# HGRN input projections: the load of the first half of the value weights moved ahead of the last three gate tiles in SyncE's queue

## The reference

```python
def prep(hh):
    p = (hh @ w_in).astype(jnp.float32)
    q, zf, zb, i, g = jnp.split(p, [HG_F, 2 * HG_F, 3 * HG_F, 3 * HG_F + HG_V], axis=-1)
    ff = lb[0] + (1.0 - lb[0]) * jax.nn.sigmoid(zf)
    fb = lb[1] + (1.0 - lb[1]) * jax.nn.sigmoid(zb)
    ...
q, i, g, (lf, kf), (lbk, kb) = prep(h)
```

## Time and profile before

| | |
|---|---|
| median of 3 runs | 2569.86 us (2567.46 to 2570.39) |
| the profiled execution | 2569.05 us |
| its span, first to last instruction | 2567.3 us |
| mean granted TensorE clock over the span | 0.988 |
| PE busy over the span | 2343.3 us, 91% |
| DMA over the span | 949.72 MB, mean 370 GB/s |

### The profile page before, as it was taken

The page is one execution under the profiler, slowest core; times in us unless marked ns, Lnnn a source line. Parts: engine busy times, 40 slices in busy tenths (PEclk is TensorE's granted clock), DMA queues, the critical chain, the costliest instruction groups (busy, mean ns, idle before and its releaser), DMA issues. The chain is left out here.

```text
span 2567.3 us, 25469 instructions
## 1 busy us (share of the span) xinstructions
PE 2343.3 (91%) x7682; PEld 1277.6 (50%) x7682; DVE 1729.9 (67%) x4248; ACT 1154.5 (45%) x3146; POOL 884.3 (34%) x802
## 2 busy tenths in 40 slices
PE   9999999999998999899999998899999888888786
PEld 4787445543553434454545444478755433333222
DVE  4866988876667666757676766564547666666665
ACT  2352568754545444534444444411424444444444
POOL 0000444443444434434444444100114444444442
PEclk9999999999999999999999999999999999999999
DMA  9433999999999999999999999595069999999997
GB/s 370 139 106 113 417 425 426 408 426 427 404 425 427 426 426 414 427 426 426 425 419 424 426 425 427 225 368 205 30 240 391 427 427 427 427 426 427 427 426 320
DMA packets 146682, 949.72 MB, mean 370 GB/s; under 512 B 16496, under 2 KB 22128, under 8 KB 44272
## 3 DMA queue, kind: packets, MB, share of 16 engines
q0 software_dynamic: 112608, 834.72, 77.6%
q1 hardware_dynamic: 33936, 113.37, 11.9%
HBM read 946.98 MB, written 1.05 MB: 369 GB/s over the span
## 5 line engine op out<-in xcount | busy, mean ns | idle before, releaser
L1123 PE MATMUL pY<-uv,diag 128*128 128x512 f32 x3072 | 1450.0, 609 | 183.0 <-ACT diag L1201 181.8
L1356 DVE SCALAR_TENSOR_TENSOR uv<-uv,H 128x1024 f32<-128x1024 f32 x768 | 939.8, 1224 | 559.9 <-DMA uv<-uv_dram,idx 558.5
L1005 POOL DMA_INDIRECT uv<-uv_dram,idx x768 | 862.4, 1123 | 1279.6 <-PE pY L1123 1087.1
L1123 PEld LDWEIGHTS pY<-uv,diag 128*128 128x128 f32 x3072 | 556.3, 191 | 948.7 <-issue 507.3
L1193 ACT ACTIVATE gelu<-dots 128x1 f32<-128x1 f32 x768 | 154.9, 202 | 891.9 <-DVE uv L1356 890.5
L1201 ACT ACTIVATE diag<-cst,coef 128x128 f32<-128x128 f32 x768 | 308.4, 402 | 72.1 <-ACT coef L1197 1.5
L1197 ACT ACTIVATE coef<-gelu,gate 128x1 f32<-128x1 f32 x768 | 226.3, 295 | 28.1 <-ACT gelu L1193 0.4
L1028 PE MATMUL pqs<-hT,wring 128*128 128x256 f32 x512 | 115.6, 379 | 0.7 <-ACT S L1176 0.7
L127 PE MATMUL plh<-hT,wring 128*128 128x256 f32 x512 | 112.5, 380 | 1.6 <-PEq L71 1.6
L1028 PEld LDWEIGHTS pqs<-hT,wring 128*128 128x128 f32 x512 | 97.2, 190 | 26.8 <-issue 15.2
L127 PEld LDWEIGHTS plh<-hT,wring 128*128 128x128 f32 x512 | 96.7, 190 | 15.9 <-issue 2.9
(11 more groups left out here) (450 smaller groups left out, 2145.2 us busy)
## 6 DMA issues: line engine op xcount, KB each, us to landing
wring<-peer_q_dram SPq DMA_DIRECT2D x36, 512.0 KB, 11.4
arena<-ada_w_dram POOLq DMA_DIRECT2D x8, 2048.0 KB, 10.7
wring<-w_in_dram SPq DMA_DIRECT2D x24, 512.0 KB, 3.6
aw<-ada_w_dram POOLq DMA_DIRECT2D x6, 2048.0 KB, 9.9
uv<-uv_dram,idx POOLq DMA_INDIRECT x768, 14.7
arena<-ada_w_dram SPq DMA_DIRECT2D x12, 1024.0 KB, 9.1
arena<-hg_zz_dram SPq DMA_DIRECT2D x16, 512.0 KB, 7.9
wring<-hg_zz_dram SPq DMA_DIRECT2D x16, 512.0 KB, 8.5
```

The source lines that it names most:

```text
L1005: nc.gpsimd.indirect_dma_start(out=uv[:, n % SLOTS, :], out_offset=None, in_=t[f"uv{l}"], in_offset=bass.IndirectOffsetOnAxis(ap=idx[:, s ...
L1123: last = nc.tensor.matmul(pY[:, b, half * 512:(half + 1) * 512], diag[:, n % DIAGS, :], uv[:, n % SLOTS, D + half * 512:D + (half + 1) * 512],
L1356: v.scalar_tensor_tensor(out=uv[:, j, 0:D], in0=uv[:, j, 0:D], scalar=1.0, in1=H2[:, own, :], op0=ALU.mult, op1=ALU.mult, accum_out=dots[: ...
```

## The change

The load of the first half of `wi` is issued behind gate tile 12, the thirteenth, and ahead of tiles 13, 14 and 15. Nothing else is different.

```diff
                 @block.sync
                 def _(sp):
-                    for i in range(RING, 16):
+                    for i in range(RING, 13):
                         load_tile(sp, "hg_zz", i, first[5] + i)
                     sp.dma_start(wi[:], t["hg_i"][:, :, 0:512]).then_inc(s_wi, 16)
+                    for i in range(13, 16):
+                        load_tile(sp, "hg_zz", i, first[5] + i)
                     lin_ahead(sp, 5)
```

## The result

| | before | changed |
|---|---|---|
| median | 2568.81 us (10 runs, 2565.09 to 2571.32) | 2575.72 us (10 runs, 2574.29 to 2578.91) |
| span of the profiled execution | 2567.3 us | 2574.6 us |
| ratio to the kernel before | | 1.0032, 95% interval 1.0024 to 1.0040 |

The ratio is +8.2 us (6.2 to 10.3); the two medians of the table stand 6.9 us apart. The change is slower by more than the 0.2% of a measurement. I had put the likeliest value at +4.7 us, slower by over 0.2% at 0.47, and a change of at most 0.2% either way at 0.50.

The account below looks back on a forecast made before the run. TensorE's chain was taken to bound the phase, with DMA scarce. Tile 13 at 1714.4 + 12.3 + 1.3 clock + 13.8 ends values(0) at 1741.8 against 1737.1: +4.7 us, forecast 2574.5 us, range 2571 to 2579.5.

Parts of the forecast that it names:

- Step 1: SP's queue: wi's last bytes out at about 1710.9, including 5.3 us for ada_w piece 3; bounds 1709.9 and 1711.9.
- Step 2: Gate tile 13 lands at 1714.4, 3.5 us behind wi's last bytes; bounds 1712.8 and 1715.4.
- rival B: DMA queues: ada_w piece 4 gets in front of tile 13, which lands at 1720.0 or later; +10 us, 2580; chance 0.15.
- the other form of B: DMA engines drain whole packets of several descriptors per ring, so tile 13 could stand behind a whole piece; within chance 0.15.
- Step 3: TensorE idles 7.8 us ahead of tile 13, lowered clock costs 1.3 us (0 to 2.5); values(0) ends at 1741.8, +4.7 us.
- Step 4: Gate tile 14 lands at 1720.1, just when TensorE asks for it: no further idle, but no reserve.
- Step 5: The other engines and loads: DVE doesn't wait for gate tiles, ada_w keeps its times, later loads cost nothing.
- a sign of being wrong: Trace after: tile 13's wait under 3 us, ada_w pieces shifting, or a later stretch taking the delay back.
- The sum: Whole kernel: +4.7 us on the profiled 2569.05 gives 2573.8; with the median 0.8 above, 2574.6, stated as 2574.5.
- Rival A: The early copy pays: tile 13 on time, gap ahead of values(0) gone, -4.4 us, 2565.5; chance 0.10.

Follow-up runs that it names:

- hold_piece3: Changed kernel, with ada_w piece 3 issued only when gate tile 13 is done; ratio 1.0031 to the kernel before.
- wide_rows_new_order: Changed kernel, with the host laying out wi in rows of 16 KB instead of 2 KB; ratio 1.0022 to the kernel before.
- wi_behind_tile14: Kernel before, with wi's first half issued behind gate tile 14, ahead of tile 15 alone; ratio 1.0013 to the kernel before.
- warm: Changed kernel, with 18 extra unused matmuls between gate tiles 12 and 13; ratio 1.0039 to the kernel before.
- wi_first: Kernel before, with wi's first half issued first in the phase's queue, ahead of gate tile 4; ratio 0.9997 to the kernel before.

## Why the prediction was right, and where its sizes were off

**The mechanism was right.** The change is slower since wi's 2.1 MB, with an ada_w piece between, stand ahead of tiles that TensorE wants sooner. The measured median, 2575.72, is in the range. That it lies only 1.2 us above 2574.5 is in part luck: the forecast stood on the 2569.86 of three runs, 1.05 above the median of ten, and the step was +4.7 forecast and +6.9 measured. To put the changed kernel's times on the clock of before I add 2.3 us.

**Step 1, wi's last bytes at 1710.9: held.** wi landed at 1710.1 + 2.3 = 1712.4; the prediction had "at about 1712.5, some 20 us behind its issue", and it was 20.0. hold_piece3 shows the part of piece 3: wi landed 5.4 us sooner without it, for the 5.3 of the sum.

**Step 2, tile 13 at 1714.4: 1.2 us short.** It landed at 1713.3 + 2.3 = 1715.6, above the high bound of 1715.4. Piece 4, issued at 1706.78, was moving bytes in the second half of 1710 to 1711, about when I had it, with tile 13 still on the way. The two queues of the changed kernel in 1710 to 1711:

```profile
q0 software_dynamic: 16, 0.26, 62.1%
q1 hardware_dynamic: 64, 0.25, 61.3%
```

That is rival B in a small dose, not its +10 us: tile 13 came 3.2 us behind wi with the piece and 1.4 us without (hold_piece3). The 3.5 us of the sum, from wi's last bytes to the landing behind them, were taken from one row, hg_qg tile 0, and that row scatters: it landed 1.9 us behind wi in the first profile of before and 4.3 in the third, so 3.2 isn't unusual, and what sets it within that spread isn't shown. A queue that gives way for a whole piece, the other form of B, is not what the traces show: 110 packets to 108 beside piece 3, in step in every us.

**Step 3, the clock at 1.3 us: the term that was mis-sized most.** Tile 13 took 6.1 us for 3.5, 2.6 us, above my upper bound of 2.5; in the other two profiles of the changed kernel it was 2.3 and 2.4. I took the price from a gap of 3.1 us behind which the clock was low for 3.4 us, and I took it short: from the first matmul of values(0) to the first of hg_qg tile 0 it is 15.5 us before and 13.8 now, so that fall had cost 1.7. Behind the 8.9 us the clock was already down when TensorE restarted and stayed down for 5 us, by this row of the changed kernel:

```profile
1713.20:1718.20 5.00, 4.90 (x12) 3.92 (x13) 3.35 (x6) 0.00 (x0) 0.53 (x1) 0.50 0.96 395
```

The length of the idle time alone doesn't give the price. In the third profile of before, values(0) took 16.3 us behind 3.2 us of it, so that the clock cost 2.4:

```profile
1718.14 16.42 PE L2684 MATMUL pi<-wi,hT 128*128 128x512 f32 x32 [3.21 <-DMA wi<-hg_i_dram]
```

Behind 6.1 and 6.5 us (wide_rows_new_order, wi_behind_tile14) it was 1.7 and 1.8, and behind 1.3 and 1.7 us (warm, hold_piece3) the clock didn't fall. One stretch was too few to price this term from.

**Step 4, tile 14 without reserve: right**, and shown by warm, where it became a wait of 0.45 us once tile 13 ran at full clock. In the changed kernel tile 14 landed at 1717.6 and was used at 1720.2, since the slow tile 13 had put TensorE back by 2.6 us.

**Step 5, "the ada_w stream keeps its times": wrong, and free.** I had looked at what DVE waits for from the loads and from the gate tiles, and left out that DVE's first product of piece 4 waits for the turn behind tile 13, which is late:

```profile
DVE h_part L2735 <- PE pmh L2674: 4.5, 2, 3.8
DVE modT L152 <- PE pmh L2674: 38.0, 1, 38.0
```

Piece 6 moved by 2.8 us (1728.78 - 1658.39 = 70.4 into the phase, 1728.27 - 1660.73 = 67.5 before), piece 7 by 0.5, and DVE's wait for the last turn, 38.0 us where it was 32.4, covers that. I had named a shift of the pieces as a sign of being wrong; it came, and cost nothing.

**The sum.** +4.7 forecast at the end of values(0), 6.65 in the pair of profiles (83.45 - 76.8), 6.5 by the means of three. The landing adds 1.2 and the clock 1.3; 0.6 go back, because I had read the end of values(0) as 1737.1 where the next matmul starts at 1737.5, and the 12.3 us from tile 13 to values(0) are 12.1 at full clock. The other 1.6 up to 8.1 lie outside the phase, at L1637. "What is added should reach the end one for one" was true for what the phase lost, but the chain behind it has a clock of its own.

**Rival A** was right about one thing, that the early copy pays, and wrong about this place. wi_first gets the whole gap back, and the Trainium skill's advice to issue early (DMA: Bandwidth & Descriptors, "Rules for kernel authors") holds there, where the DMA engines were nearly idle (a share of 0.01 from 1658 to 1664 in the kernel before), though the kernel as a whole gained nothing by it; wi_behind_tile14 and the change itself show it failing where they were full.

## What to carry to other kernels

In a queue served in order, moving a load forward is paid by every load that it passes, with its own bytes and with whatever another queue pushes in meanwhile; price the passed ones first, by when each is wanted. Put a bulk load where the DMA engines are idle, not where its consumer is near, and look at the next load of the same size on the same queue: a gap that is closed early brings that one forward too, and can be paid back there in full. A wait of TensorE can cost a stretch at 1.2 GHz on top of its length, and that price is best taken as a range: here nothing behind waits of 1.3 and 1.7 us, and 1.7 to 2.6 behind those of 2.5 to 9.6, with 1.7 and 2.4 both seen behind one of about 3.

## What the runs showed of the hardware

Two queues on the same DMA engines sent packets in step whatever their size, 110 of 2 KB to 108 of 16 KB, so that the queue of short rows got about a ninth of the bytes while the other was busy (0.23 of 2.00 MB); with rows of 16 KB in both it got 0.38 of 0.84. Alone, rows of 16 KB moved at 0.42 MB/us and rows of 2 KB at 0.29 to 0.32. The same 32 small matmuls, with no difference in their instructions, took 3.5 to 6.3 us from first to last start according to where in them the clock fell, and each kernel that was profiled three times kept to its own side of 5 us.
